# Two transformer blocks on one core: the second mixer's projection groups, its preparation and its column halves in another order

## What is computed

```python
def hybrid_layer(x, ...):
    x = x + 0.5 * swiglu(rms_norm(x, ffn1_norm), ffn1_w_in, ffn1_w_out)     # 1024 -> 2 x 2816 -> 1024
    h = rms_norm(x, mix_norm)
    proj = h @ w_mix_in                                                     # 256 x 2072
    q_a, q_b = 8 heads of 64 each, rms-normed per head, times 1/8
    k_a, v_a = 2 heads of 64; o_a = banded_attention(q_a, k_a, v_a, window 128, with sinks)
    kv_b = 6 pairs of heads: k_c, v_c (compressed), k_s, v_s, k_w, v_w
    kv_c = silu(windows of 32 tokens, stride 16, @ cmp_w1 + b1) @ cmp_w2 + b2   # 15 keys
    o_cmp, o_sel, o_win = attention of q_b over compressed, selected, window keys
    o_b = gates[0] * o_cmp + gates[1] * o_sel + gates[2] * o_win            # gates: sigmoid of 24 columns
    x = x + concat(o_a, o_b) @ w_mix_out
    x = x + 0.5 * swiglu(rms_norm(x, ffn2_norm), ffn2_w_in, ffn2_w_out)
    return x
```

## Time and profile before

| | us |
|---|---|
| median of 3 runs (lowest, highest) | 1291.36 (1286.93, 1295.63) |
| the profiled execution, its own time | 1286.68 |
| its span, first to last instruction | 1284.7 |
| PE busy | 1116.7 |
| DVE busy | 751.8 |
| ACT busy | 613.5 |

### The profile page before, as it was taken

One profiled execution on the slowest core, in us unless ns is written; L12 is line 12 of the kernel. 1 busy time (PEld: TensorE's weight loads), 2 busy tenths in 40 slices (PEclk: granted clock), 3 DMA queues, 4 the chain that ended last, 5 costly groups with the idle time before them and its releaser, 6 DMA issues.

```text
span 1284.7 us, 13977 instructions
## 1 busy us (share of the span) xinstructions
PE 1116.7 (87%) x5375; PEld 922.1 (72%) x5375; DVE 751.8 (59%) x846; ACT 613.5 (48%) x708; POOL 35.9 (3%) x44
## 2 busy tenths in 40 slices
PE   5999676768699999999877999995998878999997
PEld 4788555656577777777656788884887766788886
DVE  4444227763658778788775555565456544555553
ACT  5454450032277777877765344333444424444431
POOL 0000024200000000000000000000000000000000
PEclk8999875898589999999997999996968859999999
DMA  8755130023168898999983565663251002655520
GB/s 287 268 193 190 44 98 1 17 98 121 66 211 309 309 343 312 319 336 313 328 297 105 190 194 179 215 230 99 98 179 51 1 1 67 197 195 185 180 92 33
DMA packets 116436, 223.29 MB, mean 174 GB/s; under 512 B 6118, under 2 KB 12381, under 8 KB 116382
## 3 DMA queue, kind: packets, MB, share of 16 engines
q1 hardware_dynamic: 115698, 221.02, 50.4%
q0 software_dynamic: 368, 1.21, 0.3%
q10 hardware_dynamic: 316, 0.31, 0.1%
HBM read 221.45 MB, written 1.07 MB: 173 GB/s over the span
## 4 chain that ended last, share of the span: by engine, by line
PE 71%; DVE 16%; ACT 7%; issue 4%; ACTq 1%; POOL 0%; DMA 0%; DVEq 0%
PE ps L1448 16%; PE ps L1449 16%; PE ps L1450 16%; DVE w_lo L812 6%; PE ps L1689 4%; ACT w_hi L496 4%; PE ps L1690 4%; PE ps L1903 2%; PE ps L1715 2%; PE ps L1735 1%; PE ps L1858 1%; DVE h_lo L839 1%; DVE arena L944 1%; DVE y_lo L1181 1%; ACT y_hi L684 1%
## 5 line engine op out<-in xcount | busy, mean ns | idle before, releaser
L812 DVE TENSOR_TENSOR w_lo<-w_raw,w_hi 128x2048 fp32r<-128x2048 f32 x204 | 465.3, 2288 | 253.0 <-ACT w_hi L496 252.8
L496 ACT ACTIVATE w_hi<-w_raw 128x2048 fp32r<-128x2048 f32 x204 | 388.5, 1913 | 301.9 <-PE ps L1450 262.5
L1448 PE MATMUL ps<-w_hi,h_hi 128*128 128x512 f32 (+1 forms) x720 | 280.9, 390 | 22.2 <-DVE h_lo L839 12.2
L1449 PE MATMUL ps<-w_lo,h_hi 128*128 128x512 f32 (+1 forms) x720 | 278.8, 387 | 0.0
L1450 PE MATMUL ps<-w_hi,h_lo 128*128 128x512 f32 (+1 forms) x720 | 278.0, 386 | 0.0
L1448 PEld LDWEIGHTS ps<-w_hi,h_hi 128*128 128x128 f32 x720 | 138.8, 193 | 51.3 <-DVE h_lo L839 13.4
L1450 PEld LDWEIGHTS ps<-w_hi,h_lo 128*128 128x128 f32 x720 | 138.7, 193 | 27.1
L1449 PEld LDWEIGHTS ps<-w_lo,h_hi 128*128 128x128 f32 x720 | 138.6, 193 | 26.0
L1448 PE MATMUL ps<-w_hi,aT_hi 128*128 128x512 f32 x176 | 69.4, 394 | 7.7 <-DVE aT_lo L1093 6.0
L1449 PE MATMUL ps<-w_lo,aT_hi 128*128 128x512 f32 x176 | 69.0, 392 | 0.0
L1450 PE MATMUL ps<-w_hi,aT_lo 128*128 128x512 f32 x176 | 69.0, 392 | 0.0
(11 more groups left out here) (321 smaller groups left out, 1421.2 us busy)
## 6 DMA issues: line engine op xcount, KB each, us to landing
w_raw<-in_ffn_w_in SPq DMA_DIRECT2D x44, 1024.0 KB, 5.2
w_raw<-in_w_exp_gate SPq DMA_DIRECT2D x32, 1024.0 KB, 5.3
w_raw<-in_w_exp_up SPq DMA_DIRECT2D x32, 1024.0 KB, 6.6
w_raw<-in_w_exp_down SPq DMA_DIRECT2D x32, 1024.0 KB, 7.6
w_raw<-in_w_in SPq DMA_DIRECT2D x22, 1024.0 KB, 6.0
w_raw<-in_ffn_w_out SPq DMA_DIRECT2D x22, 1024.0 KB, 5.0
w_raw<-in_w_mix_in SPq DMA_DIRECT2D x8, 1024.0 KB, 5.1
w_raw<-in_w_out SPq DMA_DIRECT2D x4, 1024.0 KB, 5.0
```

The costliest lines, as they stand in the source:

```text
L496: act.activation(w_hi[:, u % SPLIT, :], w_raw[:, u % RAW, :], ACT.Copy).then_inc(hi_ready, 1)
L812: dve.tensor_tensor(w_lo[:, u % SPLIT, :], w_raw[:, u % RAW, :], w_hi[:, u % SPLIT, :], ALU.subtract).then_inc(lo_ready, 1)
L1448: pe.matmul(out, hi, w_h, start=first, stop=False)
L1449: pe.matmul(out, hi, w_l, start=False, stop=False)
```

## The change

Projection groups come in the order 2, 0, 1, 3, with two pairs of banks instead of four. The preparation is cut up and stands between the units. Gates are computed transposed (24 matmuls of 256 columns with the gate weights as the stationary side) and turned back. q is written once per branch, half by ACT and half by DVE; a logits matmul contracts over the 64 rows of its head. Norms and transposes of the keys of kinds 1, 2 and 3 stand between items 0 and 9, the transposes of o_a's columns between items 13 and 18, one weight split at step 27. Logits rotate through 3 banks. The output product goes by row halves first, so that its first two units need o_a alone. FFN1's and FFN2's last product, the residual and the final store go by column halves. Loads of compression weights and bias tiles are issued by ACT after FFN1's rms, no longer by SP.

The core of the diff:

```diff
...
+MIX_ORDER = (2, 0, 1, 3)
+OA_STEP0, OA_STEP1 = 13, 17
+OA_BANKS = (3, 3, 4, 5)
+SQ_WIDTH = (256, 512, 512, 384)
...
-        qqT_even = region(4096, 2, 4, S)
...
+        qT2 = region(4096, 2, 4, S)
+        k_dup = [region(7680, TT, 2 * P), proj[:, :, 0:2 * P], proj[:, :, 2 * P:4 * P]]
...
-        sq = region(8192, TT, 2048)
+        sq = [tok[:, :, 512 * n:512 * n + 512] for n in range(2)]
...
-            sp.wait_ge(ss_ready, 3)
-            sp.dma_start(cmp_w1, a["cmp_w1_2"][0].rearrange("k (pp q) h -> q k pp h", q=P)).then_inc(cmp_in, 16)
-            sp.dma_start(cmp_w2, a["cmp_w2_2"][0].rearrange("k q d -> q k d")).then_inc(cmp_in, 16)
...
+                g, kh = MIX_ORDER[(u - U_MIX) // 2], (u - U_MIX) % 2
...
+            for kh in range(2):
+                for half in range(2):
+                    load(U_MIXOUT + 2 * kh + half, unit_src(a["w_mix_out_2"][0], 512 * kh, 512 * half))
+            ffn(U_FFN2, "ffn2_w_in_2", "ffn2_w_out_2")
...
-            sp.wait_ge(blk_summed, 1)
-            sp.wait_ge(bias_stored, 32)
...
-                sp.dma_start(bias_t[:, n], bass.AP(bias_rows, n * HEADS * REL_W, [[1, P], [REL_W, HEADS], [1, S]])).then_inc(bias_in, 16)
...
+            act.dma_start(cmp_w1, a["cmp_w1_2"][0].rearrange("k (pp q) h -> q k pp h", q=P)).then_inc(cmp_in, 16)
+            act.dma_start(cmp_w2, a["cmp_w2_2"][0].rearrange("k q d -> q k d")).then_inc(cmp_in, 16)
+            act.wait_ge(bias_stored, 32)
+            for n in range(2):
+                act.dma_start(bias_t[:, n], bass.AP(bias_rows, n * HEADS * REL_W, [[1, P], [REL_W, HEADS], [1, S]])).then_inc(bias_in, 16)
...
+            split_hi(U_MIX + 3)
+            leave_mix(0)
+            split_hi(U_MIX + 4)
+            split_hi(U_MIX + 5)
+            leave_mix(1)
+            split_hi(U_MIX + 6)
+            head_rms(0, 16, 2)
+            split_hi(U_MIX + 7)
+            act.wait_ge(gates_T, 2)
...
+                ins = act.activation(gate_sig[:, tt, :], ps[:, 5, S + 32 * tt:S + 32 * tt + GATE_COLS], ACT.Sigmoid, scale=post[:, tt:tt + 1])
...
+            leave_mix(2)
+            split_hi(U_MIX + 8)
+            head_rms(16, 24, 3)
+            split_hi(U_MIX + 9)
+            act.wait_ge(kc_set, 1)
...
+            q_out_hi(0, 1)
+            leave_mix(3)
+            q_out_hi(1, 3)
...
+            head_rms(24, 30, 4)
...
+                if n == OA_STEP0:
+                    transposed_hi(5, banks=OA_BANKS, steps=(0,))
+                if n == OA_STEP1:
+                    transposed_hi(5, banks=OA_BANKS, steps=(1,))
+                if n == 3 * HEADS + 2:
+                    split_hi(U_MIXOUT + 2)
...
+                dve.wait_ge(down_half, phase)
+                add_half(0, adds)
+                dve.wait_ge(down_added, adds + 2)
+                half_done()
...
+            split_lo(U_MIX + 3)
+            split_lo(U_MIX + 4)
+            sum_blocks(0)
...
+            split_lo(U_MIX + 5)
...
+            dve.wait_ge(gates_T, 1)
+            dve.tensor_copy(gate_T, ps[0:GATE_COLS, 5, 0:S]).then_inc(gateT_set, 1)
+            sum_blocks(1)
+            split_lo(U_MIX + 6)
...
+            inv_rms(0, 16, 1)
+            scale_heads(0, 8, 8).then_inc(q_normed, 1)
+            split_lo(U_MIX + 7)
...
+            split_lo(U_MIX + 8)
+            sum_blocks(2)
+            inv_rms(16, 24, 2)
+            scale_keys(0, OFF_KA, 16)
+            scale_heads(OFF_QB, 20, 4)
+            scale_heads(OFF_QB + 256, 0, 4).then_inc(q_normed, 1)
+            dve.wait_ge(kvc_ready, 1)
...
+            dve.wait_ge(gates_T, 3)
...
+            q_out_lo(0, 1)
...
+            split_lo(U_MIX + 9)
+            k_out(0, 2, 5)
+            q_out_lo(1, 3)
+            sum_blocks(3)
...
+                if s == 0:
+                    norm_keys()
+                if s == 2:
+                    norm_cmp()
+                if s == 4:
+                    k_out(1, 4, 3)
+                if s == 7:
+                    k_out(2, 5, 3)
+                if s == 9:
+                    kcT_out()
+                if s == OA_STEP0 + 1:
+                    transposed_lo(5, banks=OA_BANKS, steps=(0,))
+                if s == OA_STEP1 + 1:
+                    transposed_lo(5, banks=OA_BANKS, steps=(1,))
+                if s == 3 * HEADS + 3:
+                    split_lo(U_MIXOUT + 2)
...
+            residual(0, U_MIXOUT + 2, (0, 1))
+            x_half()
...
+            transposed_lo(6, ROW_FFN2, banks=(4, 5, 6, 7), steps=(0, 1))
+            residual(1, U_MIXOUT + 3, (2, 3))
+            x_half()
+            transposed_lo(6, ROW_FFN2, banks=(4, 5, 6, 7), steps=(2, 3))
...
+            pe.wait_ge(tok_ready, 9)
+            transpose_cols(x, ident, (0, 1))
+            pe.wait_ge(tok_ready, 10)
+            transpose_cols(x, ident, (2, 3))
...
+            pe.wait_ge(hT_lo, 18)
+            mix_unit(0, 0)
...
-            for g in range(4):
-                unit(U_MIX + 2 * g, (2 * g, 2 * g + 1), 0, True, False)
-                unit(U_MIX + 2 * g + 1, (2 * g, 2 * g + 1), 4, False, True)
...
+            mix_unit(0, 1)
+            mix_unit(1, 0)
+            mix_unit(1, 1)
+            pe.wait_ge(mix_out, 1)
...
+            pe.wait_ge(wr_split_lo, 2)
+            for k in range(KT):
+                i = product(ps[0:GATE_COLS, 5, 0:S], wr_hi[:, k, :], wr_lo[:, k, :], h_hi[:, k, :], h_lo[:, k, :], k == 0, k == KT - 1)
+            i.then_inc(gates_T, 1)
+            pe.wait_ge(mix_out, 2)
+            mix_unit(2, 0)
+            pe.wait_ge(gateT_set, 1)
+            for tt in range(TT):
+                i = pe.transpose(ps[:, 5, S + 32 * tt:S + 32 * tt + GATE_COLS], gate_T[:, tt * P:(tt + 1) * P], ident[0:GATE_COLS, 0:GATE_COLS])
+            i.then_inc(gates_T, 1)
...
+                    i = pe.matmul(ps[:, 4, 64 * kv:64 * kv + 3 * N_CMP], cmp_w1[:, kv, pp, :],
...
+            mix_unit(2, 1)
+            pe.wait_ge(mix_out, 4)
+            mix_unit(3, 0)
...
+            pe.matmul(ps[:, 5, 384:384 + TT * GATE_COLS], flip, gate_sig.rearrange("p t c -> p (t c)"), start=True, stop=True).then_inc(gates_T, 1)
+            pe.wait_ge(q_normed, 1)
+            transpose_q(0)
+            mix_unit(3, 1)
+            pe.wait_ge(k_normed, 2)
+            pe.wait_ge(gate_flip_set, 1)
+            transpose_k(0, 5)
+            pe.wait_ge(q_normed, 2)
+            pe.wait_ge(q_set, 2)
+            transpose_q(OFF_QB)
...
-                if n >= 4:
-                    pe.wait_ge(neg_ready, n - 3)
+                r = slice((h % 2) * DH, (h % 2 + 1) * DH)
+                if n >= 3:
+                    pe.wait_ge(neg_ready, n - 2)
...
+                    keys = kkT[r, k0 + g, 0:w] if kind < 3 else kcT[r, g, 0:w]
+                    i = pe.matmul(o, qT2[r, qi, ct, qt * P:(qt + 1) * P], keys, start=True, stop=True)
...
+                if s == 4:
...
+                    transpose_k(1, 3)
+                if s == 7:
...
+                    pe.wait_ge(k_set, 2)
+                    transpose_k(2, 3)
+                if s == HEADS:
+                    pe.wait_ge(q_set, 4)
+                    pe.wait_ge(k_set, 2)
+                if s == 9:
+                    pe.wait_ge(kcn_ready, 4)
+                    pe.wait_ge(k_set, 3)
+                    for g in range(2):
+                        i = pe.transpose(ps[:, 3, 16 * g:16 * g + N_CMP], kc_n[0:N_CMP, g].rearrange("p a d -> p (a d)"), ident[0:N_CMP, 0:N_CMP])
+                    i.then_inc(kcT_T, 1)
+                if s == OA_STEP0:
+                    pe.wait_ge(kcT_set, 2)
+                    pe.wait_ge(o_used, 1)
+                    transpose_cols(tok, flip, (0,), OA_BANKS)
+                if s == OA_STEP1:
+                    pe.wait_ge(hT_lo, 21)
+                    transpose_cols(tok, flip, (1,), OA_BANKS)
...
+            pe.wait_ge(neg_ready, 4 * HEADS)
+            pe.wait_ge(hT_lo, 22)
+            unit(U_MIXOUT, (0, 1), 0, True, False)
+            pe.wait_ge(tok_ready, 12)
+            transpose_cols(tok, flip, (2, 3), OA_BANKS)
+            unit(U_MIXOUT + 1, (2, 3), 0, True, False)
...
-            square_product(U_MIXOUT)
-            transpose_tok(6)
-            pe.wait_ge(hT_lo, 28)
...
+            unit(U_MIXOUT + 2, (0, 1), 4, False, True)
+            def first_half():
+                pe.wait_ge(tok_ready, 13)
+                transpose_cols(x, ident, (0, 1), (4, 5, 6, 7))
+            unit(U_MIXOUT + 3, (2, 3), 4, False, True, inside=first_half)
+            pe.wait_ge(tok_ready, 14)
+            transpose_cols(x, ident, (2, 3), (4, 5, 6, 7))
+            pe.wait_ge(hT_lo, 26)
+            ffn(U_FFN2, N_EXP + FFN_FULL + 1, adds + 4, 28)
```

306 lines of the change are left out of this document (153 added, 153 removed).

## The result

The changed kernel takes 1306.76 us (median of 4 runs, 1301.68 to 1307.62), the kernel before beside it 1289.14 (median of 4, 1286.20 to 1295.63). The ratio is 1.012, 95% interval 1.009 to 1.015: the change makes the kernel 1.2% slower, where 1269 (1259 to 1280) was forecast. The profiled execution has a span of 1304.7 us against 1284.7.

A forecast was written before the change was run, and what follows sets the result against it. PE idle or at 1.2 GHz in four stretches of the second block's mixer and seams was taken as the bound; -3.2 - 13.9 + 5.7 - 9.2 - 1.3 = -21.9 us from the median 1291.4 gave 1269, range 1259 to 1280.

The forecast's parts named there:

- Rival C: Items run at 1.2 GHz, 1.55 us more each, +28 us if all ran low, giving 1297; chance 0.06.
- The sign set in advance: Items: the forecast is wrong if kind 0's items keep a distance over 1.8 us.
- Items, the +5.7: First exp to last values: inserted PE and DVE work, partly hidden, costs 5.7 us, range 0 to +10; 64-row logits cost 0.
- The insertion at step 27: Items: the weight split of 2.29 us straight ahead of `keep_kind`, for which PE waits already, costs 1.8 us.
- Seam 1: FFN1's end to the projection: halved additions let the first unit start at 892.0 instead of 895.2, -3.2 us.
- Projection and preparation: Projection start to first exp: preparation between units, PE never waiting there, takes 70.3 us instead of 84.2, -13.9 us.
- rival B: Gain given back in handling: insertions in the items add +4.8, five projection hand-overs +6, giving 1280; chance 0.25.
- The compression: In the projection: 24 records fast, 40 slow after the clock falls, 11.5 us, and 2.0 more for the unit behind.
- rival A: The compression stays at 2.4 GHz, 7.4 us with nothing behind it, 6.1 us more gain, giving 1263; chance 0.17.
- Loads: FFN1's start: four transfers on ACT hold the splits behind them; costed at nothing, up to 2 us without cover.
- Last values to FFN2: Last values to FFN2's first unit: the output product starts at once and the seam shortens, 30.4 instead of 39.6, -9.2 us.
- the end: Kernel's end: two of the four last additions lie under PE's second half, -1.3 us.

The follow-up runs named there:

- a_rows128_again: A second run of the changed kernel with logits over 128 rows again, all else of the change kept: 1269.46 us, ratio 0.983 to the kernel before.
- a_rows128: The changed kernel with only its 64-row logits undone (128 rows again, q written twice, masked): 1266.85 us, ratio 0.985 to the kernel before.
- after_halves: The changed kernel, 64-row logits kept, with the compression in two halves of 32 records: 1304.36 us, ratio 1.010 to the kernel before.
- a_rows128_halves: The changed kernel with 128-row logits, and the compression in two halves of 32 records, each behind its own unit: 1259.71 us, ratio 0.976 to the kernel before.
- b_rows64_twice: The kernel before with logits over 64 rows, each such matmul issued twice in a row, writing the same values again: 1345.05 us (one run).
- a_halves_late64: The changed kernel with the compression in halves, logits over 128 rows in the first kind and 64 in the other three: 1292.70 us (one run).

## Why the prediction was wrong

**The step that failed** is one sentence in the part on the items: "So half the rows make it neither cheaper nor dearer, and I take 0", with the bound that even half or double the price changes an item by 0.36 to 0.71. It asked how long one 64-row matmul lasts and never what clock is granted to a stream of them. By itself the matmul is indeed only a little dearer (0.85 against 0.71 for four). But with all logits over 64 rows PE stays at 1.2 GHz: an item takes 3.58 us in place of 1.65. Undone it gives 38.3 us of the stage back (115.69 to 77.40), done alone it costs the kernel before 41.1 in the stage (69.03 to 110.09). In the whole, the ratio to the kernel before went from 1.012 to 0.985 (0.983 in `a_rows128_again`), 34 to 37 us, and by the edit alone from 1286.20 to 1330.36, 44 us. What in a stream of 64-row matmuls keeps the clock down stays open.

**Rival C** described this outcome, items at 1.2 GHz, at 1297, and I gave it 0.06. I looked for the cause in longer idle stretches and argued it away by the idle of before. An idle stretch is where the clock fell, but not why it stayed down: `a_rows128` has all these waits and a clock of 0.79. The argument, that before "the clock came back within three items after each wait for `keep_kind`", was also misread. After the third wait it did not come back for the whole last kind, with PE busy all the time. Window of the kernel before:

```profile
1034.00:1048.00 14.00, 14.00 (x60) 10.83 (x59) 5.18 (x32) 2.73 (x16) 0.00 (x0) 0.50 0.00 1
```

The trace of before thus held a stretch of smaller matmuls (7 and 15 keys) that never raised the clock, and I did not use it. The sign set in advance, kind 0's items over 1.8 us apart, is what came. The rival's price was low as well: 28 us counted 1.55 for some 18 items, but all 24 wide items took 3.58, not 3.20, which is 9 more. With the 8.4 of `a_rows128` that makes 45 of the 46.7 us. The range, 1259 to 1280, left this case out.

**Items, the +5.7.** Within its range of 0 to 10: 77.40 - 69.03 = 8.4 in `a_rows128`. The insertion at step 27, costed at 1.8, was the largest and under-sized: moving the split gave 3.1. DVE's moved pieces, called 8.3, sum to 7.7 by their own terms, and 7.7 more is what DVE did. The bank rotation bound nothing, as said: after the change no logits matmul waited for DVE's minimum.

**Seam 1** was right by its own steps. After the split the additions go two and two, the transposes start after the first two, and from the split's start (889.29) to the first unit (896.97) it is 7.68 us, where the earlier trace rows have 10.78: 3.1 us less.

**Projection and preparation** gained 16.7, forecast 13.9. That PE would not wait between units was right: it was busy without a gap for 65.7 us, to the end of the first three items' logits at 962.7. So rival B's hand-overs did not come. The 2.8 us are mostly in PE's own work, 63.8 us to the last transposes of q where 66.4 was forecast. Eight units took 45.3: I had taken 45.2 from before, which holds a slow start of the first unit, and added 2.0 for one behind the compression, but here the first unit began at 1.00. The wait for the first exp was 3.6, forecast 3.9. **The compression** was right in this order:

```profile
927.85 11.05 PE L2007 MATMUL ps<-arena 128*128 128x45 f32 x64
```

Windows over it, each of 4 us:

```profile
928.00:932.00 4.00, 4.00 (x33) 4.00 (x33) 2.27 (x2) 3.95 (x5) 0.00 (x0) 0.87 0.65 241
932.00:936.00 4.00, 4.00 (x21) 4.00 (x20) 0.10 (x2) 0.76 (x1) 0.00 (x0) 0.50 0.69 206
936.00:940.00 4.00, 4.00 (x17) 3.81 (x17) 0.16 (x1) 0.46 (x2) 0.00 (x0) 0.50 0.15 56
940.00:944.00 4.00, 4.00 (x16) 3.20 (x16) 0.00 (x0) 0.00 (x0) 0.00 (x0) 0.85 0.02 4
```

11.05 us where 11.5 was forecast, and the clock fell inside it with PE busy all the time, so that rival A (7.4 us) did not come. The Trainium skill's rule (TensorE: Matmul & The Clock Gate, Part 1) is that busy work keeps the upper level. These windows do not agree with it (PE busy 4.00 of 4.00 us at 0.50), and the items are the strongest case: 105.8 us of work in 115.7 never raised the clock.

**Loads.** The second transfer held ACT's queue for 6.49 us (6.04 on SP in the earlier trace rows) and the two of the bias tiles 3.01 more. ACT stood idle 10.32 us ahead of the split behind them, where before it stood 4.83 ahead of the same split, so that split came 5.5 us later:

```profile
694.01 6.49 ACTq L726 DMA_DIRECT2D arena<-in_cmp_w  x1
700.54 3.01 ACTq L729 DMA_DIRECT2D arena<-bias_rows  x2
703.66 1.92 ACT L494 ACTIVATE w_hi<-w_raw 128x2048 fp32r<-128x2048 f32 x1 [10.32 <-PE ps L1569]
```

Nothing was lost by it, as costed: from FFN1's first unit to its last split on DVE both kernels take 199.74 us.

**Last values to FFN2** (-10.2, forecast -9.2) and **the end** (-1.5, forecast -1.3) were right.

## What to carry to other kernels

Leaving out work that is multiplied by zero can cost time on TensorE: here full 128-row matmuls with half of the rows masked made the items 38 us shorter than the 64-row ones that compute the same, because with a stream of the smaller matmuls the engine stayed at half its clock (0.50) while it was busy. When a change makes matmuls smaller (fewer rows or columns) anywhere between dense stages, price the stage at both clocks and give the lower one a real chance, whatever one such matmul lasts by itself. And try to cut a long run of narrow matmuls into pieces between dense units: here it saved 2.8 us in place (1.0 in `after_halves`), and with 128-row logits another 6.4 later for a reason that stays open.

## What the hardware showed unexpectedly

- A clock of 0.50 from 965 to the end of the items at 1080, with PE busy for 105.8 of the stage's 115.7 us; with 64 rows in half of the heads it averaged 0.77.
- Two identical waits, two clocks. PE waits 2.60 us for `keep_kind` in `a_rows128_again` and in `a_rows128_halves`, after the same items; then its first instructions are

```profile
986.32 0.66 PE L2078 MATMUL ps<-arena 128*128 128x64 f32 x2 [2.60 <-DVE tok L1499]
```

```profile
985.85 0.41 PE L2083 MATMUL ps<-arena 128*128 128x64 f32 x2 [2.60 <-DVE tok L1499]
```

the first at 1.2 GHz, the second at 2.4. It was so in three traces of the one kind and in three of the other. The kernel before has both in one trace: waits of 2.60 us ahead of its second and of its third kind, with the clock at 0.50 at the end of the first wait (first values 0.66 us) and at 1.00 at the end of the second (0.41), to fall 1 us later. Why cutting the compression 45 us earlier should decide it stays open; that it moves where in time the waits fall would be one way, and was not tried.
- The same 64-row logits run at either clock: at 1.00 in the first kind of `b_rows64_twice` and at the start of `a_halves_late64`, at 0.50 after the first wait for `keep_kind` in both.
